# Expert items with their gathered turns on both sides of the activations' turn, and the q/k norm's sums and root among the value projections

## The reference, cut to what matters

```python
def l2norm(x):
    xf = x.astype(jnp.float32)
    return xf * lax.rsqrt(jnp.sum(xf * xf, axis=-1, keepdims=True) + NORM_EPS)

    # gdn_branch: short causal conv and silu, then the norm of q and k per head
    qkv, new_buf = short_conv(qkv, conv_buf, lw['conv_w'])
    q, k, v = jnp.split(qkv, [GDN_QK_W, 2 * GDN_QK_W], axis=-1)
    q = l2norm(q.reshape(Bn, T, GDN_HEADS, GDN_DK)) * GDN_DK ** -0.5
    k = l2norm(k.reshape(Bn, T, GDN_HEADS, GDN_DK))

    # moe_ffn, for each of 32 experts (top 4 of 32 per token)
        gu = xb @ lw['w_gu'][e] + lw['b_gu'][e]
        gt = jnp.minimum(gu[:, :D_EXPERT], SWIGLU_LIMIT)
        up = jnp.clip(gu[:, D_EXPERT:], -SWIGLU_LIMIT, SWIGLU_LIMIT)
        act = (up + 1.0) * gt * jax.nn.sigmoid(SWIGLU_ALPHA * gt)
        return act @ lw['w_dn'][e] + lw['b_dn'][e]
```

## Time and profile before

| | before |
|---|---|
| runs, median of 3 (range) | 1619.71 us (1619.17 to 1627.57) |
| the profiled execution's own time | 1616.13 us |
| its span, first to last instruction | 1614.3 us |
| TensorE busy | 1543.7 us (96%) |
| VectorE, ScalarE busy | 480.2 us (30%), 342.7 us (21%) |
| HBM read | 533.54 MB, 335 GB/s over the span |

### The profile page before, as it was taken

How to read it: one execution, slowest core, us unless ns; L and a number is a source line. 1 busy time by engine, 2 the same in 40 slices (tenths; PEclk the granted TensorE clock), 3 DMA queues, 4 the chain that set the end, 5 groups by cost and what they waited for, 6 DMA issues and landing times.

```text
span 1614.3 us, 25511 instructions
## 1 busy us (share of the span) xinstructions
PE 1543.7 (96%) x10185; PEld 845.7 (52%) x10185; DVE 480.2 (30%) x1071; ACT 342.7 (21%) x793; POOL 6.8 (0%) x13
## 2 busy tenths in 40 slices
PE   6999989999999999999999999999999999999997
PEld 4887886776677687434334333333343333333333
DVE  1566556322301025222222221222222222212224
ACT  2323452223311102111111111111111111111113
POOL 0000000000000000000000000000000000000000
PEclk9998999999999998999999999999999999999999
DMA  9749332634499965499999999999999999999991
GB/s 397 319 156 379 156 159 85 229 135 154 137 322 354 347 274 186 184 430 426 424 427 427 428 428 428 428 428 429 428 429 428 427 423 425 426 422 425 427 422 56
DMA packets 60259, 541.33 MB, mean 335 GB/s; under 512 B 7298, under 2 KB 11906, under 8 KB 29346
## 3 DMA queue, kind: packets, MB, share of 16 engines
q1 hardware_dynamic: 59474, 534.65, 80.6%
q0 software_dynamic: 720, 5.76, 0.9%
HBM read 533.54 MB, written 6.84 MB: 335 GB/s over the span
## 4 chain that ended last, share of the span: by engine, by line
PE 74%; DMA 14%; DVE 7%; issue 3%; SPq 1%; ACT 1%; ACTq 0%; DVEq 0%
PE banks L547 16%; PE banks L595 14%; DMA regC<-biases 13%; PE banks L1300 9%; PE banks L850 5%; PE banks L523 2%; PE banks L583 2%; DVE regA L683 2%; PE banks L565 2%; PE banks L510 2%; PE banks L1133 2%; PE banks L1065 2%; PE banks L795 2%; DMA ring<-wpre 1%; PE banks L949 1%
## 5 line engine op out<-in xcount | busy, mean ns | idle before, releaser
L547 PE MATMUL banks<-ring,regA 128*64 128x512 f32 x2024 | 446.9, 594 | 0.7 <-ACT regA L620 0.7
L547 PEld LDWEIGHTS banks<-ring,regA 128*64 128x64 f32 x2024 | 142.4, 137 | 281.8 <-issue 280.8
L595 PE MATMUL banks<-ring,regC 128*64 128x512 f32 x1024 | 226.8, 595 | 0.0
L657 DVE TENSOR_TENSOR regB<-regB,banks 128x528 f32<-128x528 f32 x128 | 81.5, 698 | 365.7 <-PE banks L523 365.7
L595 PEld LDWEIGHTS banks<-ring,regC 128*64 128x64 f32 x1024 | 70.7, 137 | 131.8 <-issue 127.9
L623 ACT ACTIVATE regA<-regA 128x512 f32<-128x512 f32 x32 | 20.2, 630 | 516.2 <-DVE regA L678 516.2
L678 DVE TENSOR_SCALAR regA<-banks 128x512 f32<-128x512 f32 x32 | 22.1, 691 | 335.7 <-PE banks L565 335.7
L496 PE MATMUL banks<-regC,regA 128*64 128x512 f32 (+1 forms) x396 | 98.7, 616 | 0.0
L850 PE MATMUL banks<-hT,ring 128*128 128x264 f32 x384 | 86.0, 387 | 0.0
L850 PEld LDWEIGHTS banks<-hT,ring 128*128 128x128 f32 x384 | 72.8, 190 | 12.4
L523 PE MATMUL banks<-regA,regC 64*128 64x264 f32 x512 | 71.6, 409 | 0.0
(11 more groups left out here) (476 smaller groups left out, 1628.5 us busy)
## 6 DMA issues: line engine op xcount, KB each, us to landing
ring<-w_gu SPq DMA_DIRECT2D x126, 2048.0 KB, 16.3
ring<-w_dn SPq DMA_DIRECT2D x64, 2048.0 KB, 13.9
ring<-wpre SPq DMA_DIRECT2D x41, 2048.0 KB, 12.9
ring<-kvT SPq DMA_DIRECT2D x64, 256.0 KB, 4.7
ring<-kv SPq DMA_DIRECT2D x64, 256.0 KB, 6.0
ring<-ssm SPq DMA_DIRECT2D x2, 2048.0 KB, 9.8
o_ssms<-ring POOLq DMA_DIRECT2D x2, 2048.0 KB, 7.4
regC<-w_gu SPq DMA_DIRECT2D x1, 2048.0 KB, 9.5
```

Of the source, the lines that this page charges most:

```text
L547: mm = pe_mm(bank[x // 2][SLOT * (x % 2):SLOT * (x % 2 + 1), :], lhsT=hg[:, k % 4, SLOT * (k // 4):SLOT * (k // 4 + 1)], rhs=weights_k[:, ...
L595: mm = pe_mm(bank[5][SLOT * y:SLOT * (y + 1), :], lhsT=actT[:, m % 4, SLOT * (m // 4):SLOT * (m // 4 + 1)], rhs=ring[c][:, D * (m % 4) + H ...
L657: V.tensor_tensor(pair, pair, banks[:, b:b + 2, 0:T], ALU.add).then_inc(acc_added, 1)
```

## The change

In stage one the prompt's sums stand in the projection loop ahead of tile 20 and the samples' sums ahead of tile 21; the root follows on ACT at `m` = 20, the reciprocal on DVE at `m` = 21. The samples' convolution is split into q and k (inside the loop) and v (behind it); the reading of the gate logits and their sigmoid move to `m` = 2 and 3. Behind the loop the 16 spreads go in four groups of four between the modulation pieces, in banks 4 to 7. In stage two the first two of `turn_gathered`'s four matmuls go ahead of the activations' turn, the other two stay behind it. SP issues item 2's first chunk into `ring0` as soon as item 0 has read it, and its loop is cut between chunk 0 and chunk 1. The diff's core; "..." marks what is left out:

```diff
+QK_V = (slice(0, 2 * H), slice(2 * H, 3 * H))
...
-L2_BANKS = (0, 1, 2, 3)
+L2_BANKS = (4, 5, 6, 7)
...
-            def item(j, e):
-                for c in range(RING):
-
+            def later_chunks(j, e):
+                for c in range(1, RING):
                     sp.wait_ge(moe_read, j * 6 + (c - 5))
                     load(c, e)
                 load_bias(e)
+
+            def first_chunk(j, e):
+                sp.wait_ge(moe_read, j * 6 - 5)
+                load(0, e)
 
             sp.wait_ge(ss_ready, 2)
             sp.dma_start(ahead, wgu[1, :, 0:CH]).then_inc(inputs_in, 16)
             sp.wait_ge(stage("h2_turned"), 6)
             sp.dma_start(ahead_half, wgu[1, :, CH:CH + CH // 2]).then_inc(inputs_in, 16)
+            sp.wait_ge(moe_read, 1)
+            load(0, 2)
             sp.wait_ge(moe_read, 2)
             sp.dma_start(ring[1][:, CH // 2:CH], wgu[1, :, CH + CH // 2:2 * CH]).then_inc(slot_in[1], 16)
...
+            with sp.Fori(2, NE - 1) as j:
+                later_chunks(j, j)
+                first_chunk(j + 1, j + 1)
+            later_chunks(NE - 1, NE - 1)
...
-            def turn_gathered(n):
-
-                pe.wait_ge(gtok_copied, n)
-                for q in range(4):
+            def turn_gathered(first, last):
+                for q in range(first, last):
                     mm = pe_mm(bank[3][:, P * q:P * (q + 1)], lhsT=gtok[:, P * q:P * (q + 1)], rhs=ident, start=True, stop=True)
-                mm.then_inc(g_turned, 1)
+                return mm
...
+                pe.wait_ge(gtok_copied, j + 2)
+                turn_gathered(0, 2)
                 pe.wait_ge(act_ready, j + 1)
                 for y in range(2):
-                    if y == 1:
-                        pe.wait_ge(gtok_copied, j + 2)
                     for q in (2 * y, 2 * y + 1):
                         mm = pe_mm(bank[4 - 2 * y][:, P * q:P * (q + 1)], lhsT=act_[:, P * q:P * (q + 1)], rhs=ident, start=True, stop=True)
                     mm.then_inc(a_turned, 1)
-                turn_gathered(j + 2)
+                turn_gathered(2, 4).then_inc(g_turned, 1)
...
+                if m == 2 * H + 4:
+                    pe.wait_ge(l2sq, 2 * H)
+                    for i in range(2 * H):
+                        mm = pe_mm(group_sum(i, slice(0, NPR)), lhsT=row_sum(i // 4, 4), rhs=sqb[:, i, :], start=(i < 4), stop=(i >= 2 * H - 4),
+                                   skip_group_check=True)
+                    mm.then_inc(l2ss, 1)
+                if m == 2 * H + 5:
+                    pe.wait_ge(l2sq, 2 * H + 1)
+                    for i in range(2 * H):
+                        mm = pe_mm(group_sum(i, slice(NPR, T)), lhsT=row_sum(i // 4, 4), rhs=sq_s[:, i, :], start=(i < 4), stop=(i >= 2 * H - 4),
+                                   skip_group_check=True)
+                    mm.then_inc(l2ss, 1)
...
-            pe.wait_ge(l2sq, 2 * H)
-            for i in range(2 * H):
-                mm = pe_mm(group_sum(i, slice(0, NPR)), lhsT=row_sum(i // 4, 4), rhs=sqb[:, i, :], start=(i < 4), stop=(i >= 2 * H - 4),
-                           skip_group_check=True)
-            mm.then_inc(l2ss, 1)
-            pe.wait_ge(proj_evac, CONVT)
...
+            def spreads(first):
+
+                for i in range(first, first + 4):
+                    spread(i)
+
             pe.wait_ge(stage("l2_rs"), 1)
...
+            pe.wait_ge(stage("ab_copied"), 1)
+            spreads(0)
+            pe.wait_ge(proj_evac, CONVT)
+            modulate(4, 0)
+            modulate(5, 1)
+            turn_mod(4, 2)
+            spreads(4)
+            pe.wait_ge(mod_row, 5)
+            modulate(6, 0)
...
+            pe.wait_ge(bg_done, 1)
+            pe.wait_ge(l2done, 2 * H - 1)
...
+            pe.wait_ge(mod_row, 8)
+            modulate(9, 1)
+            pe.wait_ge(mod_evac, 7)
+            turn_mod(8, 2)
...
+                    if g == 0 and c == 0:
+                        pe.wait_ge(l2done, 2 * H)
+                    if g == 1 and c == 0:
+                        pe.wait_ge(mod_evac, MOD_PRE)
...
+                        pe.wait_ge(mod_evac, 8)
+                        turn_mod(9, 3)
                         pe.wait_ge(*once("cum_read"))
                         pe.wait_ge(stage("egB_ready"), 1)
-                        pe.wait_ge(l2done, 2 * H)
-                        pe.wait_ge(mod_evac, MOD_PRE)
...
+            def sample_sigmoid(part):
+
+                act.wait_ge(stage("conv_s"), part + 1)
+                r = QK_V[part]
+                A(smt[:, 1, r, :], smt[:, 0, r, :], ACT.Sigmoid).then_inc(once(("qk_sig", "v_sig")[part])[0], 1)
...
+                if m == 3:
+                    act.wait_ge(stage("ab_copied"), 1)
+                    A(beta_tok[:, :, :], gsc[:, 0, :, :], ACT.Sigmoid).then_inc(ab_act, 1)
+                if m == 2 * H + 2:
+                    sample_sigmoid(0)
+                if m == 2 * H + 3:
+                    act.wait_ge(*once("qk_silu"))
+                    A(sq_s[:, :, :], qkvT[:, 0:2 * H, NPR:T], ACT.Square).then_inc(l2sq, 1)
+                if m == 2 * H + 4:
                     act.wait_ge(l2ss, 2)
                     A(rsb[:, 0, :], bank[5][:, 0:T], ACT.Sqrt, scale=1.0, bias=con[:, C_EPS:C_EPS + 1]).then_inc(root_ready, 1)
...
+            mod_rows(4, 0)
+            sample_sigmoid(1)
+            mod_rows(5, 1)
...
+            mod_rows(6, 0)
             A(gsc[:, 2, :, :], gsc[:, 2, :, :], ACT.Ln, bias=1.0).then_inc(ab_act, 1)
-            for i in range(2):
-                mod_rows(MOD_BACK + i, 4 + i)
+            mod_rows(7, 1)
+            mod_rows(8, 0)
...
+            mod_rows(9, 1)
...
+            def sample_conv(part):
+
+                r = QK_V[part]
+                n = r.stop - r.start
+                for j in range(4):
+                    dst = smt[:, 0, r, :] if j == 0 else smt[:, 1, r, :]
+                    link(V.tensor_tensor(dst, samp[:, r, j, :], convw[:, r, j:j + 1].to_broadcast([P, n, NSA]), ALU.mult))
+                    if j:
+                        ins = V.tensor_tensor(smt[:, 0, r, :], smt[:, 0, r, :], smt[:, 1, r, :], ALU.add)
+                        if j < 3:
+                            link(ins)
+                        else:
+                            ins.then_inc(stage("conv_s"), 1)
+
+            def sample_silu(part):
+
+                r = QK_V[part]
+                dve.wait_ge(*once(("qk_sig", "v_sig")[part]))
+                V.tensor_tensor(qkvT[:, r, NPR:T], smt[:, 0, r, :], smt[:, 1, r, :], ALU.mult).then_inc(once(("qk_silu", "v_silu")[part])[0], 1)
...
+                if m == 2:
...
+                if m == 2 * H + 1:
+                    sample_conv(0)
+                if m == 2 * H + 2:
+                    sample_silu(0)
...
+                if m == 2 * H + 5:
                     dve.wait_ge(root_ready, 2)
                     V.reciprocal(rsb[:, 0, :], rsb[:, 0, :]).then_inc(stage("l2_rs"), 1)
+            sample_conv(1)
...
+                if i == 3:
+                    sample_silu(1)
+                    mod_bias(4, 2)
+                if i == 11:
+                    mod_bias(5, 3)
...
+            mod_bias(6, 2)
...
+            mod_bias(7, 3)
...
+            mod_bias(8, 2)
+            mod_bias(9, 3)
```

More of the change, by code:

```diff
@@ L434, in number_of_items, with for_items @@
             return eng.value_load(items[0:1, 0:1], min_val=NE, max_val=NJ)
-        def for_items(eng, first, item, further=None):
+        def for_items(eng, first, item):
             with eng.Fori(first, NE) as j:
@@ L443, in for_items @@
                     with eng.If(j < K):
-                        (further or item)(j)
+                        item(j)
             return K
@@ L486, in moe_loads @@
             load_bias(1)
-            def further(j):
-                item(j, sp.value_load(items[0:1, bass.ds(j + 1, 1)], min_val=0, max_val=NE - 1))
-            for_items(sp, 2, lambda j: item(j, j), further)
+            with sp.Fori(2, NE - 1) as j:
+                later_chunks(j, j)
+                first_chunk(j + 1, j + 1)
+            later_chunks(NE - 1, NE - 1)
+            K = number_of_items(sp)
+            with sp.If(K > NE):
+                with sp.Fori(NE, NJ) as j:
+                    with sp.If(j < K):
+                        e = sp.value_load(items[0:1, bass.ds(j + 1, 1)], min_val=0, max_val=NE - 1)
+                        first_chunk(j, e)
+                        later_chunks(j, e)
         def moe_tensor(pe, more_selections, more_products):
@@ new lines, in _ @@
+            pe.wait_ge(stage("ab_copied"), 1)
[7 more added lines that the diff above has]
+            modulate(6, 0)
+            turn_mod(5, 3)
+            spreads(8)
+            pe.wait_ge(mod_row, 6)
+            modulate(7, 1)
+            pe.wait_ge(mod_evac, 5)
+            turn_mod(6, 2)
+            spreads(12)
+            pe.wait_ge(mod_row, 7)
@@ new lines, in _ @@
+            modulate(8, 0)
+            pe.wait_ge(mod_evac, 6)
```

(11 more changed lines are left out.)

94 lines of the change are left out of this document (17 added, 77 removed).

## The result

The changed kernel takes 1612.63 us (median of 7 runs, 1607.87 to 1615.54) beside 1619.47 us of the kernel before (7 runs): a ratio of 0.9947, 95% interval 0.9932 to 0.9963, so 8.6 us (6.0 to 11.0) less; the two medians themselves lie 6.8 us apart. Twelve more runs in a later series gave 1613.04 us and 0.9960 (0.9939 to 0.9981). The forecast was 1611.7 us, 8.05 less. Its profiled execution took 1608.53 us, with a span of 1606.7; before it was 1616.13 and 1614.3, so 7.6 us lie between the two traces.

A forecast was written before the change was run, and what follows sets the result against it. Bound: stage one by TensorE's chain with a 3.98 us hole, stage two by the DMA's 29.71 us per item. Stage one -5.45, early chunk -2.1, turn -0.5: -8.05 from 1619.71 gives 1611.7 us, range 1605 to 1616.5.

The forecast's parts named there:

- The hole goes: Stage one, between projections and spreads: root and reciprocal run beside tiles 20 to 23, -3.98 us; sums and turns add 1.63.
- The products' low clock goes: Stage one, first four product groups: 5.40 us becomes 4 x 0.89, -1.84 us, if the hole caused the low clock.
- The modulation piece's low clock goes: Stage one, a modulation piece behind the projections: 3.57 to 1.88 us, -1.69, if the hole caused the low clock.
- the first rival: Stage one, second group of spreads: the clock falls once more, costing 2.26 us, so 1613.9 us; chance 0.17.
- The spreads' waits: Stage one, spreads waiting for DVE: 1.62 us at the second group, about 0.75 at the fourth; spreads +0.43 in all.
- The stall of 0.85, left standing: Stage one, TensorE's stall at 132.14 us without a releaser: kept in the forecast, its end counted as the upper bound.
- All later work of stage one and two is released by TensorE's own progress, so it moves along: Behind stage one's first products: the whole stage-one gain of 5.45 us is carried on to later work.
- The turn: Stage two, ahead of the activations' turn: two gathered turns fill 0.50 us of TensorE's wait, counted once behind the last biases.
- The early chunk, 2.1: Stage two, item 2's first chunk issued at about 655 instead of 686 us: gains 2.1 us once, bounds 0 and 4.95.
- From there the DMA is full in both kernels: Stage two, from item 2's `w_dn` landing at 715.46 instead of 717.56 us: the gain stays 2.1 us.
- The DMA is at its end: Stage two: the DMA needs 29.71 us per item whatever TensorE's pace; the opposing rival, 1592.9 us, had chance 0.05.
- both middle rivals: Stage one's clock falls once more (1613.9 us, chance 0.17) and early chunk only shifts idle time (1613.8, 0.13); together 1616.2.

The follow-up runs named there:

- stage one alone: The kernel before with only the change's stage-one edits, stage two as it was: 1616.59 us, ratio 0.9964 to the kernel before.
- the chunk alone: The kernel before with only SP's early issue of item 2's first chunk, turns as they were: items take 913.95 us, beside 914.48 before.
- the one with the turn: The whole change without the early issue of item 2's first chunk, gathered turns still on both sides: 1615.43 us, ratio 0.9964 to the kernel before.
- both runs that took work away: The whole change with, from item 2 on, half of each scatter's columns (items 912.27 us) or half of the second `w_dn` chunk (items 895.70, run 1593.98 us).
- the run with less work for TensorE: The whole change, but from item 2 on each scatter writes 132 of 264 columns: items take 912.27 us, 0.15 less than with the whole change.

## Why the prediction came out, step by step

- **The hole goes:** right. No piece of ACT or DVE for the root stands between projections and products.
- **The products' low clock goes:** right, 4 x 0.89.
- **The modulation piece's low clock goes:** wrong; it was the first rival. The piece takes 2.85 us in place of 1.88, two turns 0.73 (0.42) and a group of spreads 0.95 (0.69): 1.5 us, where the rival was priced at 2.26. Of the ten traces with the new stage one, the seven with the wait ahead of the second group have this fall right behind it, the three without the wait don't.
- **The spreads' waits:** the second group cost 0.77 idle and 2.09 - 0.69 = 1.40 more, so 2.17 where 1.62 was worked out; the fourth 1.48 - 0.69 = 0.79 where it was 0.75.
- **The stall of 0.85, left standing:** it did not come back ahead of the products, which pays for much of this (0.83 us of stall stands behind them, at 160.84). So 4.53 us at the end of the sum, forecast 5.45.
- **"All later work of stage one and two is released by TensorE's own progress, so it moves along":** this step failed. The stretch behind the products took 4.3 us more, because the DMA did not move along: the state's loads were asked for sooner, the weights ahead of them were not done sooner, and TensorE came sooner to code whose packet came through the same full DMA.
- **The turn:** right. Behind the last bias matmuls it gives 30.51 - 30.06 = 0.45 us (forecast 0.50), and in the loop TensorE's 0.43 per item counts only until the DMA binds.
- **The early chunk, 2.1:** half of it failed. The term was 1.0 for two shorter items and 1.1 for a DMA no longer behind. In the profiled pair the items did gain 7.15 - 5.10 = 2.05 us, but that is luck: the same item code takes 914.48 us in the trace of before and 913.09 with stage one alone. The items take 913.8 us on the mean of the three traces that have neither edit or the chunk alone, 912.85 in the one with the turn, 912.5 on the mean of the seven with both: about 1.0 for the turn, as worked out, and 0 to 0.4 for the chunk, from few traces. The step that failed is "From there the DMA is full in both kernels": its lower bound, "0, if the DMA idles as long as it gained", is what happened, since the binding chunk was not item 2's `w_dn` but each one after it.
- **The DMA is at its end:** right, by both runs that took work away. The ceiling of 435 GB/s in the Trainium skill ("DMA: Bandwidth & Descriptors", "Where 436 GB/s comes from") would have left 0.8 us per item, which the run with less work for TensorE did not find. That 29.71 "holds to 0.01" was read from one pair; over the late items of that trace it is 29.66 to 29.71.
- **The range's upper end:** both middle rivals together come to 1616.0, not 1616.2; nothing hangs on it.

What makes the sum fit none the less: in the profiled pair the clock fell in the router stage before and not after, 3.6 us. That code is the same in both. In the other eleven traces the fall is there in eight and absent in three, whatever the kernel, so this part is chance in a pair of traces. Over many runs the clock still favours the change. The 63 runs of the kernel before in the later series have a mean granted clock of 0.9889 and 1620.67 us, and the line through them falls by 1.29 us for each 0.001. The 12 later runs of the whole change have 0.9917 and 1612.96, the 17 of the kernel before beside them 0.9895 and 1619.77: of 6.8 us, 0.0022 x 1290 = 2.8 go with the clock. For stage one alone it is 0.9912 and 1615.10 beside 0.9887 and 1620.57, 3.2 of 5.5. Part of this the two profiles show: before, the clock is low at 136 to 143 us and again in the products, after at 133 to 137 and behind the stall at 178 to 181. Why it falls less often elsewhere too stays open.

So the forecast was right in its total, and only partly in its reasons: stage one was sized too large by about 5 us and the early chunk by about 1, and in the profiled pair a router stage without a fall of the clock (3.6), a shorter stall near 223 us (1.2) and slow items in the trace of before, which no step of the sum named, stood in for them.

## What to carry to other kernels

A gain in front of a queue of transfers is not a gain behind it: when TensorE's wait goes, ask which loads will now be asked for sooner, what stands ahead of them and behind them in the DMA, and order the loads by when they are needed, not by when a buffer is free. A chunk fetched early helps a DMA-bound loop only if the next buffers come free sooner as well; otherwise the DMA idles later for what it gained. And a total that fits in one pair of traces proves little where the clock alone moves a run by several us: follow the lead from place to place.

## What the runs showed of the hardware

- TensorE stands still without a releaser for up to 3.60 us where weights are queued, and not at all at that place where none are, with the same code. Each of 39 such stalls in the thirteen traces ends 1.22 to 1.55 us behind a 16 KB packet of the instruction queue q8, on which the page counts 47 packets and 0.77 MB. The Trainium skill, "Runtime: NRT & Kernel Launch", "Instruction fetch mechanics", says that code is refilled by DMA in 16 KiB blocks and that the cost of crossing a block is mostly hidden. The size agrees, and so does "mostly": 196 of the 235 packets between 118 and 250 us have no stall behind them. With weights queued a refill need not be hidden: at the block products it cost 1.07 to 3.60 us in the ten traces with loads queued. The Trainium skill, "DMA: Bandwidth & Descriptors", "Queues, rings and completion order", lets the DMA engines take turns between queues, by which a refill would wait for one packet and not for the queue. In these traces a long stall is one whose packet begins late: 1.04 us ahead of the stall's start for the 1.36 us before, 1.23 us behind it for the 3.60 us after. Why it begins late no run here tells.
- Behind the second group of spreads, 2.09 us that trickle behind DVE, the granted clock fell to 0.50, seven times in seven; in the three traces without that wait it did not fall there.
- Half the columns in a scatter did not halve it: such a record takes 299 ns in place of 409, and what is saved goes in part into waits for DVE.
